# Order of the first stage, the sums of squares and the ones row in a two-layer hybrid encoder step on one Trainium2 core

## The chip, the cores and the metric

The program runs on one core of a Trainium2 chip. The core has TensorE (matrix products, two clock levels, 1.2 and 2.4 GHz), VectorE, ScalarE, GpSimd and SyncE (which issues transfers), an on-chip memory of 128 partitions (SBUF), and an accumulator memory of eight banks (PSUM) that TensorE writes. The metric is device microseconds of one execution.

## The reference

One inference step of two layers for 16 meta tokens, 1024 prompt tokens and 32 sample tokens. Shortened, one layer is:

```python
z = rmsnorm(x, norm_mix_g) @ w_in
c_q, c_kv, k_r, x_r, g_r = split(z)           # 768, 256, 32, 512, 512 columns
q = rmsnorm(c_q, q_norm_g) @ w_uq             # 8 heads of 64 + 32; the 32 are rotated
ckv, kpe = rmsnorm(c_kv, kv_norm_g), rope(k_r)
xc = conv_b + sum(shifted(x_r, k) * conv_w[k] for k in range(4))
r, i = sigmoid(xc @ w_gate_a + b_gate_a), sigmoid(xc @ w_gate_x + b_gate_x)
a = exp(-8 * r * softplus(-lam))
h_t = a_t * h_(t-1) + sqrt(1 - a_t**2) * i_t * xc_t
y = h * gelu(g_r)
o = softmax(q @ keys, chunk-causal) @ values  # keys and values from ckv, kpe and the past
x = x + concat(rmsnorm(o, attn_out_g), rmsnorm(y, lru_out_g)) @ w_out
x = x + square(relu(rmsnorm(x, norm_mlp_g) @ w_up)) @ w_down
```

After the second layer a last rmsnorm gives the outputs; new latent rows, rotary keys and states are outputs too.

## The kernel before

The 1074 columns (1072 tokens and two of padding) stand in the free dimension throughout: x is eight tiles of 128 x 1074 (`xall`). A product with K = 1024 is made from eight tiles k. Each float32 operand is split into a high and a low half, and each product runs three passes (high by high, high weight by low x, low weight by high x) over three chunks of 358 columns: 72 matmuls (`product`, L525).

Weights come in blocks of 128 x 1024. SyncE loads block b into `raw[b % 2]` (512 KB), ScalarE copies it to `whi[b % 2]` (`split`, L766) and VectorE subtracts to get `wlo[b % 2]` (L1079 in the layer's first part, L1452 in the MLP). The products are numbered units; unit u writes PSUM slot u % 2 (three banks), and may start only when unit u - 2 has been read (`take` and the table `READ`). Every engine's program is one list written by hand; engines meet only at counted semaphores. SyncE's list is a queue too: a transfer that waits holds all behind it.

A layer runs in this order. (1) A sum of squares of x: TensorE multiplies the summed squares `msq` by a tile of ones (`norm_sum`, L538), ScalarE takes the root (`root`), VectorE the reciprocal (`rstd`, L1083); every sum is a unit of its own and takes a slot. (2) Products XR0 to XR3, each followed on VectorE by `scaled` (PSUM times the reciprocal, L1089) and a convolution (L1105 to L1111). (3) Gate products (`gates`, 2 x 9 matmuls for each of four tiles c), between them GR0 to GR3 (inputs of gelu), CKV0, CKV1, KR and CQ0; for each tile VectorE runs `xc_lo`, `lru` (a reciprocal L1125, two scans L1133 and L1134), and `gelu`, with a cube on GpSimd. (4) CQ1 to CQ5, then their low halves (`lo`, L1096), then UQ0 to UQ5 (54 matmuls each), of which the last two are the rotary ones (`rotate`). (5) Keys (K, four units of 18 matmuls) and values (V, L627). (6) Eight heads in two slots of operands, even and odd (`qe`, `keh`, `kel`; `qo`, `koh`, `kol`): row maxima (L602), which become a row of shifts carried to the operands by transfers (`qe<-mt`), scores (L669), exponentials on ScalarE (L958), and products with the values (L654). VectorE's copies for head h + 2 are `load_hi` (L1317); the lru group's norm (`y_root`, `y_norm`) lies in heads 0 and 1. A row of ones in the keys multiplies the shift row; GpSimd sets it, and zeros around it, in each slot (L1553, L1575, L1577). (7) Output products OY0 to OY7 (36 matmuls, from y), a sum of squares between the third and the fourth, then OO0 to OO7 (from attention). (8) MLP, four groups of 16 units; in the last, x's tiles get their next halves `xgh` (L1032), `xgl` and squares.

The sum of the MLP's norm already lies outside the slots before: in PSUM banks 6 and 7 and in the rest of a slot.

## Time and profile before

| | us |
|---|---|
| median of 3 runs | 2854.16 |
| the three runs | 2854.16, 2854.26, 2852.26 |
| the profiled execution | 2850.93 |
| its span, first to last instruction | 2848.9 |
| TensorE busy | 2684.7 (94%) |
| VectorE busy | 1303.5 (46%) |
| ScalarE busy | 813.6 (29%) |
| mean granted clock of TensorE | 0.979 |

Busy time is time in which an engine runs an instruction; for TensorE it doesn't tell at which clock. Times in the rows below count from the span's start. Engines are named PE, DVE, ACT, POOL and SP there, L525 is a line of the kernel, "x360" a count of instructions, and names stand without buffer numbers.

### The profile page before, as it was taken

How to read it: one execution, taken by the hardware profiler on the slowest of the kernel's cores; microseconds unless marked ns; L12 is line 12 of the kernel's file. 1: busy time of each engine (PE TensorE's matmuls, PEld its weight loads, DVE VectorE, ACT ScalarE, POOL GpSimd, SP SyncE). 2: the span in 40 equal slices, each digit the busy share in tenths (PEclk: the TensorE clock that was granted, in tenths of full speed). 3: DMA queues.
4: the chain of work that ended last, by engine and by line, in shares of the span. 5: the costliest groups of instructions: out<-in, count | busy, mean ns of one | idle time of the engine just before them, and what ended most of it. 6: DMA issues, size and time to landing. Idle time of an engine off the chain costs nothing.

```text
span 2848.9 us, 37082 instructions
## 1 busy us (share of the span) xinstructions
PE 2684.7 (94%) x15742; PEld 2582.5 (91%) x15742; DVE 1303.5 (46%) x1425; ACT 813.6 (29%) x1235; POOL 353.1 (12%) x230
## 2 busy tenths in 40 slices
PE   6899989999999999999999998899999999999995
PEld 5889967899999999999989887778999999999995
DVE  7785666565223223223378855764542232222334
ACT  3342245533202112022223333454321120220221
POOL 0022243211000000000201323341200000000011
PEclk9999999999999999999999999999999999999998
DMA  5111200211111111111221111002111111111122
GB/s 189 45 51 57 68 9 18 79 56 49 45 45 45 45 45 45 45 45 58 80 69 45 63 45 53 9 33 78 52 45 45 45 45 45 46 45 45 45 76 93
DMA packets 46114, 152.48 MB, mean 54 GB/s; under 512 B 8849, under 2 KB 10033, under 8 KB 45953
## 3 DMA queue, kind: packets, MB, share of 16 engines
q1 hardware_dynamic: 38576, 128.69, 13.8%
q0 software_dynamic: 5792, 15.86, 1.4%
q10 hardware_dynamic: 1584, 5.54, 0.5%
q8 instruction: 132, 2.16, 0.3%
q14 instruction: 30, 0.24, 0.0%
HBM read 127.48 MB, written 20.24 MB: 52 GB/s over the span
## 4 chain that ended last, share of the span: by engine, by line
PE 85%; DVE 6%; ACT 3%; issue 2%; POOL 2%; DMA 2%; SPq 0%; DVEq 0%; ACTq 0%; POOLq 0%
PE ps L725 53%; PE ps L525 20%; PE ps L654 5%; PE ps L669 4%; PE ps L602 2%; DVE t L1125 1%; PE ps L627 1%; PE ps L538 1%; POOL t L1520 1%; DMA qo<-mt 0%; DVE wlo L1079 0%; DVE xc L1133 0%; DMA comp<-sum_scratch 0%; DVE xc L1111 0%; ACT t L786 0%
## 5 line engine op out<-in xcount | busy, mean ns | idle before, releaser
L1452 DVE TENSOR_TENSOR wlo<-raw,whi 128x1024 fp32r<-128x1024 f32 x124 | 151.9, 1225 | 901.0 <-ACT whi L1019 900.9
L1019 ACT ACTIVATE whi<-raw 128x1024 fp32r<-128x1024 f32 x124 | 131.5, 1060 | 973.1 <-PE ps L725 972.8
L725 PE MATMUL ps<-xmh,whi 128*128 128x358 f32 x1536 | 336.2, 327 | 2.7 <-issue 2.7
L725 PE MATMUL ps<-xml,whi 128*128 128x358 f32 x1536 | 336.8, 327 | 0.0
L725 PE MATMUL ps<-fh,whi 128*128 128x358 f32 x1536 | 336.4, 327 | 0.0
L725 PE MATMUL ps<-fh,wlo 128*128 128x358 f32 x1536 | 336.3, 327 | 0.0
L725 PE MATMUL ps<-xmh,wlo 128*128 128x358 f32 x1536 | 335.5, 326 | 0.0
L725 PE MATMUL ps<-fl,whi 128*128 128x358 f32 x1536 | 335.1, 326 | 0.0
L725 PEld LDWEIGHTS ps<-xmh,whi 128*128 128x128 f32 x1536 | 264.4, 189 | 3.8 <-issue 3.8
L725 PEld LDWEIGHTS ps<-fl,whi 128*128 128x128 f32 x1536 | 266.6, 189 | 0.0
L725 PEld LDWEIGHTS ps<-fh,whi 128*128 128x128 f32 x1536 | 265.9, 189 | 0.0
L725 PEld LDWEIGHTS ps<-xmh,wlo 128*128 128x128 f32 x1536 | 265.8, 189 | 0.0
L725 PEld LDWEIGHTS ps<-fh,wlo 128*128 128x128 f32 x1536 | 265.0, 189 | 0.0
L725 PEld LDWEIGHTS ps<-xml,whi 128*128 128x128 f32 x1536 | 264.5, 189 | 0.0
L525 PE MATMUL ps<-xgh,whi 128*128 128x358 f32 x816 | 184.2, 335 | 21.8 <-ACT t L786 21.8
L1497 POOL DMA_DIRECT2D x_scratch<-xall x24 | 13.5, 562 | 1481.3 <-DVE xall L1470 1464.4
L525 PE MATMUL ps<-xgl,whi 128*128 128x358 f32 x816 | 181.6, 331 | 0.0
L525 PE MATMUL ps<-xgh,wlo 128*128 128x358 f32 x816 | 180.8, 330 | 0.0
L1328 DVE TENSOR_REDUCE mxp<-ps 64x1 f32<-64x64 f32 (+11 forms) x384 | 141.2, 372 | 84.1 <-PE ps L602 77.5
L525 PEld LDWEIGHTS ps<-xgh,whi 128*128 128x128 f32 x816 | 143.8, 194 | 25.5 <-issue 24.9
L1462 DVE TENSOR_TENSOR fl<-msq,fh 128x1074 fp32r<-128x1074 f32 x64 | 81.8, 1278 | 147.4 <-ACT fh L1027 147.4
L766 ACT ACTIVATE whi<-raw 128x1024 fp32r<-128x1024 f32 (+3 forms) x80 | 74.8, 935 | 249.5 <-PE ps L525 249.2
(260 smaller groups left out, 4034.0 us busy)
## 6 DMA issues: line engine op xcount, KB each, us to landing
raw<-in_wst SPq DMA_DIRECT2D x204, 512.0 KB, 3.3
x_scratch<-xall POOLq DMA_DIRECT2D x24, 537.0 KB, 3.8
xall<-x_scratch ACTq DMA_DIRECT2D x10, 537.0 KB, 6.2
xall<-in_xT SPq DMA_DIRECT2D x8, 537.0 KB, 8.1
out_yT<-xall SPq DMA_DIRECT2D x8, 537.0 KB, 3.7
rc<-sum_scratch SPq DMA_DIRECT2D x16, 268.0 KB, 4.0
xall<-x_scratch SPq DMA_DIRECT2D x6, 537.0 KB, 4.6
ra<-qr SPq DMA_DIRECT2D x16, 134.2 KB, 2.4
```

The source lines that it names most:

```text
L525: mm = nc.tensor.matmul(dst(q), wt, r(q), start=(k == 0 and i == 0), stop=(k == n - 1 and i == 2))
L538: mm = nc.tensor.matmul(ps[:, 3 * (u % 2) + q, 0:CH], ones[:, :], tile[:, q * CH:(q + 1) * CH], start=True, stop=True)
L602: mm = nc.tensor.matmul(ps[:, max_bank(h, s), c0:c0 + n], qs[e][0][rows, q0:q0 + P], ks[e][0][rows, k0:k0 + n], start=True, stop=True, ski ...
L627: mm = nc.tensor.matmul(ps[:, t % 3, :], (ckvh if a == "h" else ckvl)[k][:, c0:c0 + P], (whi if c == "h" else wlo)[B_UV % 2][:, 512 * k:51 ...
L654: mm = nc.tensor.matmul(ps[0:65, bank, c0:c0 + n], v[:, v0:v0 + 65], p_tile(gk)[:, 0:n], start=(k in FIRST), stop=(k in LAST))
L669: mm = nc.tensor.matmul(ps[:, gi % 3, 0:n], ks[e][0 if a == "h" else 1][rows, k0:k0 + P], qs[e][0 if c == "h" else 1][rows, q0:q0 + n], st ...
L725: mm = nc.tensor.matmul(ps[:, 3 * (u % 2) + q, 0:CH], wt, (rh if c == "h" else rl)[kk](q), start=(kk == 0 and i == 0), stop=(kk == 7 and i ...
L766: nc.scalar.activation(whi[b % 2][:, 0:n], raw[b % 2][:, 0:n], ACT.Copy).then_inc(S["w_hi"], 1)
L1019: nc.scalar.activation(whi[b % 2][:, :], raw[b % 2][:, :], ACT.Copy).then_inc(S["w_hi"], 1)
L1328: ins = V.reduce_max(mxp[lo_:hi_, tile, part:part + 1], ps[lo_:hi_, max_bank(h, s), c0:c0 + n], AX_X)
L1452: V.tensor_tensor(wlo[b % 2][:, :], raw[b % 2][:, :], whi[b % 2][:, :].bitcast(F32), ALU.subtract).then_inc(S["w_lo"], 1)
L1462: V.tensor_tensor(fl[k][:, :], msq[:, :], fh[k][:, :].bitcast(F32), ALU.subtract).then_inc(S["f_lo"], 1)
```

## The change

It has six parts. (a) In layer 0 SyncE issues x's tiles first, the first two weight blocks among them and the constants behind them; XR0 and XR1 run interleaved, tile by tile, as x's low halves come; x isn't stored at the start and is read from the input again for the residual. In layer 1 the first two blocks are loaded and split in the MLP's last group, and XR0 doesn't wait for the sum. (b) All sums of squares lie outside the slots, in banks 6 and 7 (`sum_of`), each behind another product: MIX behind XR1 (layer 0) or XR0 (layer 1), KV behind CQ1, Y behind CQ4, Q behind UQ1, O behind OY4. (c) The order is XR0 to XR3, GR0, GR1, gates 0, GR2, GR3, gates 1, CKV0, CKV1, gates 2, KR, CQ0, gates 3, CQ1 and on; the four convolution inputs have tiles of their own, `lru` is cut in two with the next tile's `xc_lo` between, the rotary query units come first, and y is normalised before attention. (d) VectorE sets the ones and zeros in the rotary keys' tile `kpe`, and they reach both slots with the copies of its rows; GpSimd's settings in the key slots go. (e) The eight transfers of rotated queries stand among the loads of blocks 28 to 30. (f) The last layer makes no next halves of x and stores no x.

The diff, cut to what the parts below speak of:

```diff
-B_XR, B_GR, B_CKV, B_KR = [0, 1, 2, 3], [5, 6, 8, 9], [11, 12], 14
-B_GATE = [4, 7, 10, 13]
-B_CQ = [15, 16, 17, 18, 19, 20]
+B_XR, B_GR, B_CKV, B_KR = [0, 1, 2, 3], [4, 5, 7, 8], [10, 11], 13
+B_GATE = [6, 9, 12, 15]
+B_CQ = [14, 16, 17, 18, 19, 20]
...
+U_XR, U_GR, U_GATE, U_CKV = [0, 1, 2, 3], [4, 5, 8, 9], [6, 10, 14, 18], [12, 13]
+U_KR, U_CQ = 16, [17, 20, 21, 22, 23, 24]
+U_UQ, U_K, U_V = [25, 26, 27, 28, 29, 30], 31, 35
+U_OY, U_OO, U_MLP = [45 + _c for _c in range(8)], 53, 61
...
+SUM_MIX, SUM_KV, SUM_Y, SUM_Q, SUM_O, SUM_MLP = 1, 2, 3, 4, 5, 6
+SUM_AT = {SUM_KV: U_CQ[1], SUM_Y: U_CQ[4], SUM_Q: U_UQ[1], SUM_O: U_OY[4], SUM_MLP: U_MLP}
...
+            for m in range(8):
+                sp.dma_start(x[m], xT[m]).then_inc(S[f"x_load{m}"], 16)
+                if m < 2:
+                    sp.dma_start(raw[m][:, :], wst[m]).then_inc(S[f"raw{m}"], 16)
             sp.dma_start(ones[:, :], ident_in[1]).then_inc(S["const_in"], 16)
             sp.dma_start(ident[:, :], ident_in[0]).then_inc(S["const_in"], 16)
             sp.dma_start(fg[:, :], fgain).then_inc(S["const_in"], 16)
...
-                w("mm", U_SMIX + 1)
+                def load(b):
+                    w("w_lo", b)
+                    sp.dma_start(raw[b % 2][:, :], wst[L * NB + b]).then_inc(S[f"raw{b % 2}"], 16)
+                if L:
+                    for n in (0, 1):
+                        sp.wait_ge(S["w_lo"], L * NB + n)
+                        sp.dma_start(raw[n][:, :], wst[L * NB + n]).then_inc(S[f"raw{n}"], 16)
+                    sp.wait_ge(S["xg_hi"], L * 8 + 8)
+                    sp.wait_ge(S["xg_lo"], L * 8 + 8)
+                    sp.dma_start(vecs[:, :], vec[L]).then_inc(S["vec_in"], 16)
+                sp.dma_start(h0s[:, :], h0[L]).then_inc(S["small_in"], 16)
+                sp.dma_start(xs[:, :, 0:CW - 1], conv0[L]).then_inc(S["small_in"], 16)
+                sp.dma_start(past[:, :, :], past_ckv[L]).then_inc(S["small_in"], 16)
+                w("sum", SUM_MIX)
                 sp.dma_start(cosT[:, :], ropeC).then_inc(S["table_in"], 16)
                 sp.dma_start(sinT[:, :], ropeS).then_inc(S["table_in"], 16)
-                with sp.Fori(1, 15) as i:
+                with sp.Fori(1, 14) as i:
...
+                def sum_of(n, tile):
+                    if n > 1 or L:
+                        pe.wait_ge(S["root"], L * PER["root"] + n - 1)
+                    for q in range(2):
+                        nc.tensor.matmul(ps[:, 6 + q, :], ones[:, :], tile[:, 512 * q:512 * q + 512], start=True, stop=True)
+                    nc.tensor.matmul(sum_rest(slot_of(sum_at(n, L))), ones[:, :], tile[:, SUM_END:T], start=True, stop=True).then_inc(S["sum"], 1)
+                pe.wait_ge(S["const_in"], 48)
...
+                if L == 0:
+                    for k in range(8):
+                        x_ready(k)
+                        for c in (0, 1):
+                            if k == 0:
+                                w("w_lo", B_XR[c] + 2)
+                            dst = to_slot(U_XR[c])
+                            for i, (a, b) in enumerate(PASSES):
+                                wt = (whi if a == "h" else wlo)[B_XR[c] % 2][:, 128 * k:128 * k + 128]
+                                for q in range(3):
+                                    mm = nc.tensor.matmul(dst(q), wt, (XH if b == "h" else XL)[k](q), start=(k == 0 and i == 0), stop=(k == 7 and i == 2))
+                            if k == 7:
+                                mm.then_inc(S["mm"], 1)
+                    mix_sum()
+                else:
+                    product(to_slot(U_XR[0]), U_XR[0], B_XR[0], 0, XH, XL, x_ready)
+                    mix_sum()
+                    product(to_slot(U_XR[1]), U_XR[1], B_XR[1], 0, XH, XL)
+                def x_product(u, b):
+                    product(to_slot(u), u, b, 0, XH, XL)
+                for c in (2, 3):
+                    x_product(U_XR[c], B_XR[c])
+                for c in (0, 1):
+                    x_product(U_GR[c], B_GR[c])
                 gates(0)
+                for c in (2, 3):
+                    x_product(U_GR[c], B_GR[c])
+                gates(1)
                 for c in (0, 1):
-                    product(to_slot(U_GR[c]), U_GR[c], B_GR[c], 0, XH, XL)
-                gates(1)
-                for c in (2, 3):
-                    product(to_slot(U_GR[c]), U_GR[c], B_GR[c], 0, XH, XL)
+                    x_product(U_CKV[c], B_CKV[c])
                 gates(2)
-                for c in (0, 1):
-                    product(to_slot(U_CKV[c]), U_CKV[c], B_CKV[c], 0, XH, XL)
+                x_product(U_KR, B_KR)
+                x_product(U_CQ[0], B_CQ[0])
                 gates(3)
-                product(to_slot(U_KR), U_KR, B_KR, 0, XH, XL)
-                product(to_slot(U_CQ[0]), U_CQ[0], B_CQ[0], 0, XH, XL)
+                x_product(U_CQ[1], B_CQ[1])
...
+                sum_of(SUM_KV, sqa)
+                for c in (2, 3, 4):
+                    x_product(U_CQ[c], B_CQ[c])
+                w("y_sum", 3)
+                sum_of(SUM_Y, t3)
+                x_product(U_CQ[5], B_CQ[5])
...
-                        if i == 3:
-                            w("o_sum", 3)
-                            norm_sum(U_SO, osq)
                         product(to_slot(U_OY[i]), U_OY[i], B_OY + bi, 512 * n, [tok(t) for t in yh], [tok(t) for t in yl],
                                 (lambda k: w("y_lo", k + 1)) if i == 0 else None)
+                        if U_OY[i] == SUM_AT[SUM_O]:
+                            w("o_sum", 3)
+                            sum_of(SUM_O, osq)
...
+                def root(n, dst, dim):
+                    w("sum", n)
+                    nc.scalar.activation(dst[:, 0:SUM_END].rearrange("p (c n) -> p c n", c=2), ps[:, 6:8, :], ACT.Sqrt, scale=1.0 / dim, bias=eps[:, 0:1])
+                    nc.scalar.activation(dst[:, SUM_END:T], sum_rest(slot_of(sum_at(n, L))), ACT.Sqrt, scale=1.0 / dim, bias=eps[:, 0:1]).then_inc(S["root"], 1)
...
+                V.memset(kpe[32:33, :], 1.0)
+                V.memset(kpe[96:97, :], 1.0).then_inc(S["kpe_ones"], 1)
...
+                    V.tensor_tensor(g[c][:, :], g[c][:, :], t3[:, :], ALU.mult).then_inc(S["y_n"], 1)
...
-                        if h == 0 and i in (14, 16, 18):
-                            y_root((i - 14) // 2)
-                        if h == 1 and i in (15, 16, 17, 18):
-                            y_norm(i - 15)
...
-                rstd(rs, 5)
+                split(32)
                 add_y(3)
-                split(32)
+                add_y(4)
+                rstd(rs, SUM_O)
+                split(33)
+                add_y(5)
                 for j in range(4):
                     V.tensor_tensor(o[j][:, :], o[j][:, :], rs[:, :], ALU.mult).then_inc(S["o_n"], 1)
-                add_y(4)
-                add_y(5)
-                split(33)
+                    if j == 0:
+                        split(34)
...
+                            if L < DEPTH - 1:
+                                nc.scalar.activation(xgh[m][:, :], x[m], ACT.Copy, scale=col(V_GNEXT + m)).then_inc(S["xg_hi"], 1)
...
-                w("mm", U_V + 10)
-                for k in range(2):
-                    G.memset(ks[1][k][32:64, :].bitcast(F32), 0.0).then_inc(S["slot1_set"], 1)
-                    w("slot1_set", 3 + k)
-                G.memset(ks[1][0][32:33, :].bitcast(F32), 1.0).then_inc(S["slot1_set"], 1)
-                w("slot1_set", 5)
+                for part in range(2):
+                    G.memset(qs[1][part][32:64, :].bitcast(F32), 0.0).then_inc(S["slot1_set"], 1)
+                    w("slot1_set", part + 1)
```

The rotary tables (`cosT`, `sinT`) are loaded behind the MIX sum in both, since `sinT` lies where the squares lay.

What the order of instructions shows. First SyncE's queue at the start; `xall` is x, `raw_49` and `raw_50` are the two buffers for weight blocks, `ones`, `ident` and `fg` the constants, `rope_87` and `rope_88` the rotary tables. Before:

```order
L406 DMA ones<-in_consts 128x128
L407 DMA ident<-in_consts 128x128
L408 DMA fg<-in_fgain 128x8
L410 DMA xall<-in_xT 128x1074 x8
L419 DMA raw_49<-in_wst 128x1024 [waits w_lo]
L419 DMA raw_50<-in_wst 128x1024 [waits w_lo]
...
L429 DMA rope_87<-in_ropeC 128x1074 [waits mm]
L430 DMA rope_88<-in_ropeS 128x1074
...
L434 DMA raw_49<-in_wst 128x1024
```

After:

```order
L425 DMA xall<-in_xT 128x1074
L427 DMA raw_49<-in_wst 128x1024
L425 DMA xall<-in_xT 128x1074
L427 DMA raw_50<-in_wst 128x1024
L425 DMA xall<-in_xT 128x1074 x6
L428 DMA ones<-in_consts 128x128
L429 DMA ident<-in_consts 128x128
L430 DMA fg<-in_fgain 128x8
...
L454 DMA rope_87<-in_ropeC 128x1074 [waits sum]
L455 DMA rope_88<-in_ropeS 128x1074
...
L459 DMA raw_49<-in_wst 128x1024
```

The constants move behind x and two blocks; the third block stays behind the tables, which wait for the sum.

Second, VectorE's list for one round of gates; `wlo` is a weight's low half, `xcs_96<-xc_74` the low half of the next convolution result, `g_82<-ps,rs` a scaled product, the reciprocal and what follows it the recurrence. Before, around the recurrence of tile 0:

```order
L1079 TENSOR_TENSOR wlo_53<-raw_49,whi_51 128x1024
L1094 TENSOR_TENSOR xcs_96<-xc_73,xcs_95 128x1074
L1124 TENSOR_SCALAR t_77<-t_76 128x1074
L1125 RECIPROCAL t_77<-t_77 128x1074
L1127 TENSOR_SCALAR t_76<-t_77 128x1074
...
L1133 SCALAR_TENSOR_TENSOR xc_72<-t_76,t_79 128x1040
...
L1079 TENSOR_TENSOR wlo_54<-raw_50,whi_52 128x256
L1089 TENSOR_TENSOR g_80<-ps,rs 128x1074
L1089 TENSOR_TENSOR g_81<-ps,rs 128x1074
L1079 TENSOR_TENSOR wlo_53<-raw_49,whi_51 128x1024
```

After:

```order
L1166 TENSOR_TENSOR wlo_53<-raw_49,whi_51 128x256
L1176 TENSOR_TENSOR g_80<-ps,rs 128x1074
L1166 TENSOR_TENSOR wlo_54<-raw_50,whi_52 128x1024
L1176 TENSOR_TENSOR g_81<-ps,rs 128x1074
L1166 TENSOR_TENSOR wlo_53<-raw_49,whi_51 128x1024
L1217 TENSOR_SCALAR t_77<-t_76 128x1074
L1218 RECIPROCAL t_77<-t_77 128x1074
L1181 TENSOR_TENSOR xcs_96<-xc_73,xcs_95 128x1074
L1223 TENSOR_SCALAR t_76<-t_77 128x1074
...
L1229 SCALAR_TENSOR_TENSOR xc_72<-t_76,t_79 128x1040
```

The scaled products of the first GR pair move ahead of the first recurrence, with a weight split between the two, and the next tile's low half moves into the recurrence.

Third, GpSimd's list around the first shift rows (`qe<-mt`); `koh` and `kol` are the odd slot's keys, `qo` its queries. Before:

```order
L1569 MEMSET qo 32x1074 [waits p_zero]
L1571 MEMSET qo 32x1074 [waits slot1_set]
L1575 MEMSET koh 32x1296 [waits mm,slot1_set]
L1575 MEMSET kol 32x1296 [waits slot1_set]
L1577 MEMSET koh 1x1296 [waits slot1_set]
L1586 DMA qe<-mt 1x2x16 [waits mt_lo,slot1_set]
L1587 DMA qe<-mt 1x2x32
```

After:

```order
L1689 MEMSET qo 32x1074 [waits p_zero]
L1689 MEMSET qo 32x1074 [waits slot1_set]
L1698 DMA qe<-mt 1x2x16 [waits mt_lo,slot1_set]
L1699 DMA qe<-mt 1x2x32
```

The three settings of the odd slot's keys, of which the first waits for the last product of V, are gone from ahead of the transfer.

## Rows read from the trace of the kernel before

**Rows 1.** The page, busy us of each engine, share of the span, instructions.

```profile
PE 2684.7 (94%) x15742; PEld 2582.5 (91%) x15742; DVE 1303.5 (46%) x1425; ACT 813.6 (29%) x1235; POOL 353.1 (12%) x230
```

**Rows 2.** TensorE's waits: what ended them, us in total, times, longest us.

```profile
PE ps L538 <- DVE msq L1061: 28.4, 1, 28.4
PE ps L525 <- ACT t L786: 21.8, 6, 7.0
PE ps L602 <- issue: 18.8, 8, 3.4
PE ps L669 <- DMA qe<-mt: 15.7, 4, 7.5
PE ps L525 <- DVE cql L1096: 13.1, 4, 3.8
```

**Rows 3.** The chain of waits: start, us, what.

```profile
2.15 4.25 DMA xall<-in_xT
...
32.21 47.53 PE ps L525 x288
...
213.41 59.31 PE ps L525 x360
...
290.16 1.81 PE ps L538 x6
291.97 44.45 PE ps L525 x270
...
386.08 1.38 PE ps L654 x2
407.50 3.38 issue
...
432.20 2.53 issue
...
576.59 2.08 PE ps L538 x6
578.67 76.93 PE ps L525 x468
...
1419.63 1.19 ACT xgh L1032
...
1475.73 1.28 DVE t L1089
```

**Rows 4.** Windows: length, busy us of five engines, granted clock, DMA share, GB/s.

```profile
281.00:285.00 4.00, 4.00 (x15) 4.00 (x16) 4.00 (x4) 4.00 (x5) 0.00 (x0) 0.57 0.02 3
149.71:180.44 30.73, 27.16 (x163) 26.64 (x163) 26.06 (x19) 14.65 (x14) 6.15 (x2) 1.00 0.16 51
290.00:338.00 48.00, 48.00 (x285) 46.68 (x283) 27.49 (x17) 11.58 (x12) 6.30 (x3) 1.00 0.17 55
```

**Rows 5.** Transfers of the first 40 us: GB/s in slices of 1 us, one issue group.

```profile
GB/s 0 32 136 134 284 412 370 408 387 266 296 309 425 421 421 425 417 412 421 410 425 414 430 411 412 425 417 421 300 26 129 0 0 159 279 412 388 369 16 0
...
raw<-in_wst SPq DMA_DIRECT2D x3, 512.0 KB, 16.9
```

**Rows 6.** Timeline of SyncE, the first rotary table's issue.

```profile
32.24 0.33 SPq L429 DMA_DIRECT2D rope<-in_ropeC  x1
```

**Rows 7.** Timeline of VectorE, recurrence of the second tile.

```profile
130.84 6.87 DVE L1125 RECIPROCAL t<-t 128x1074 f32<-128x1074 f32 x1
...
142.18 3.10 DVE L1133 TENSOR_TENSOR_SCAN xc<-t,t 128x1040 f32<-128x1040 f32 x1
145.21 2.46 DVE L1134 TENSOR_TENSOR_SCAN xc<-t,h0s,t 128x34 f32<-128x34 f32 x1
```

**Rows 8.** Timelines of GpSimd and ScalarE between values and scores.

```profile
375.54 1.74 POOL L1575 MEMSET koh<- 32x1296 f32 x1 [11.59 <-PE ps L627]
...
378.36 1.06 ACT L766 ACTIVATE whi<-raw 128x1024 fp32r<-128x1024 f32 x1
```

**Rows 9.** Timeline of VectorE, four tiles of attention output normalised.

```profile
588.59 4.83 DVE L1427 TENSOR_TENSOR o<-o,rs 128x1074 f32<-128x1074 f32 x4
```

More of the change, by code:

```diff
@@ L139 @@
 Y_AT = [3, 6, 9, 14]
-DVE_CHAIN = 82
+DVE_CHAIN = 87
 VTILES = [P * t for t in range(10)]
@@ L267, in trunk @@
         xc = tiles("xc", "F", 0, 4)
-        t1, t2, t3 = tiles("t", "F", 4, 3)
-        t4 = place("t4", "F", 7 * TB, T + 16)
+        tp = [place(f"t{i + 1}", "F", (4 + i) * TB + 64 * i, T + 16) for i in range(4)]
+        t1, t2, t3 = (tp[i][:, 0:T] for i in range(3))
+        t4 = tp[3]
+        xr = [tp[3], tp[0], tp[1], tp[2]]
         g = tiles("g", "G", 0, 4)
@@ L408, in _ @@
             sp.dma_start(fg[:, :], fgain).then_inc(S["const_in"], 16)
-            for m in range(8):
-                sp.dma_start(x[m], xT[m]).then_inc(S[f"x_load{m}"], 16)
             for L in range(DEPTH):
@@ L507, in take @@
                 def take(u):
-                    if u >= 2:
+                    if u in U_XR[0:2]:
+                        if L:
+                            pe.wait_ge(S["res_add"], L * PER["res_add"] - 1 + u)
+                        return
+                    if u == U_XR[2] and L == 0:
+                        w("xr_raw", 1)
+                    else:
                         w(*READ[u - 2])
+                    for n in range(1, 7):
+                        if sum_at(n, L) == u - 2:
+                            w("root", n)
                 def product(dst, u, b, woff, rhs_h, rhs_l, ready=None):
@@ L531, in to_slot, with mix_sum, x_ready @@
                 def to_slot(u):
[L532 to L546 removed]
+                    return lambda q: ps[:, 3 * slot_of(u) + q, 0:CH]
+                def sum_of(n, tile):
[5 more added lines that the diff above has]
+                pe.wait_ge(S["const_in"], 48)
+                XH, XL = [tok(t) for t in xgh], [tok(t) for t in xgl]
+                def mix_sum():
+                    pe.wait_ge(S["sq_sum"], L * 7 + 7)
+                    sum_of(SUM_MIX, msq)
+                def x_ready(k):
+                    w("xg_lo", k + 1)
                 def gates(c):
@@ L567, in _ @@
                 w("ckv_sum", 1)
-                norm_sum(U_SKV, sqa)
-                for c in range(1, 6):
-                    product(to_slot(U_CQ[c]), U_CQ[c], B_CQ[c], 0, XH, XL)
+                sum_of(SUM_KV, sqa)
[4 more added lines that the diff above has]
+                x_product(U_CQ[5], B_CQ[5])
                 for m in range(6):
@@ L697, in _ @@
                 FH, FL = [tok(t) for t in fh], [tok(t) for t in fl]
-                def mlp_sum():
-                    w("xm_sum", 7)
-                    for q in range(2):
-                        nc.tensor.matmul(ps[:, 6 + q, :], ones[:, :], msq[:, 512 * q:512 * q + 512], start=True, stop=True)
-                    nc.tensor.matmul(sum_rest(U_MLP % 2), ones[:, :], msq[:, SUM_END:T], start=True, stop=True).then_inc(S["mlp_sum"], 1)
                 def mlp_group(gg, first):
@@ new lines, in _ @@
+                scaled(U_KR, kpe[:, 0:T], rs, "kr_ev")
+                scaled(U_CQ[0], cq[0], rs, "cq_ev")
+                split(16)
+                gelu(2)
+                split(17)
+                lru_a(3)
+                lru_b(3)
+                w("root", SUM_KV)
+                scaled(U_CQ[1], cq[1], rs, "cq_ev")
+                split(18)
+                rstd(sqt, SUM_KV)
+                split(19)
+                scaled(U_CQ[2], cq[2], rs, "cq_ev")
+                gelu(3)
+                V.tensor_copy(hbuf[:, 3, 1:2], xc[3][:, TOK - 1:TOK]).then_inc(S["hid_out"], 1)
@@ L1230, in _ @@
                         .then_inc(S["ckv_n"], 1)
+                scaled(U_CQ[3], cq[3], rs, "cq_ev")
+                split(20)
+                w("table_in", 32)
+                w("kr_ev", 1)
+                rotate(kpe[:, 0:T], t1[:, :], "kpe_new")
                 w("ckv_n", 2)
-                scaled(U_CQ[1], cq[1], rs, "cq_ev")
                 for c in range(2):
@@ L1448, in mlp_group @@
                     for k in range(2 * GT):
-                        if not (last and k >= 2 * GT - 2):
+                        if not (last and L == DEPTH - 1 and k >= 2 * GT - 2):
                             b = B_MLP + k + 2
@@ L1497, in save_x @@
                 pool.dma_start(x_scr[m], x[m]).then_inc(S["x_out"], 16)
-            for m in range(8):
-                pool.wait_ge(S[f"x_load{m}"], 16)
-                save_x(m)
             for L in range(DEPTH):
```

479 lines of the change are left out of this document (241 added, 238 removed).

## The prediction

> **What bounds the kernel now.** I read the page first: TensorE is busy for 94% of the span [rows 1], so the kernel is a string of products with gaps, and a change of order can win only the gaps and what follows them. The view of TensorE's waits says what ends them [rows 2]: 28.4 us before the first sum of squares, 21.8 us in six waits for gate results from ScalarE, 18.8 us of "issue" (behind VectorE's copies ahead of a head), 15.7 us for the shift rows and 13.1 us for the low halves of the compressed queries. The chain of waits puts times to the stages [rows 3]. One product with K = 1024 is 72 matmuls: 59.31 us / 360 x 72 = 11.86 us; a gate product (9) is 1.48, an up-projection of queries (54) 8.9, a sum of squares at full clock 1.81. The granted clock adds to each gap: in the four microseconds from 281, right behind a gap, it was 0.57, near the lower of the two levels, 1.2 of 2.4 GHz [rows 4]. So a gap of about 3 us costs (1 - 0.57) x 4 = 1.7 us more.
>
> **Front, layer 0.** The new order puts x0 first on SP's queue and the constants behind all of x and two weight blocks. Before, x0 lands 4.25 us after its issue [rows 3]; issued at 0.76 it lands at about 5.0. Before, the bus moves 410 to 425 GB/s from microsecond 12 to 27 [rows 5]; eight x tiles and two blocks are 5.3 MB, 1.3 us each: the last x lands near 16.9, the constants at 17.2. TensorE waits for these first, so the early tiles buy no early start. That they queue behind is shown by the weight blocks of before, issued behind x: 16.9 us to landing, where 3.3 to 4 is usual [rows 5]. This speaks against the part of the change that puts x first. The Trainium skill, "DMA: Bandwidth & Descriptors", Queues, rings and completion order, speaks against it too: descriptors of one ring start in order, and only between queues does an engine take turns. By it the constants would come at 17.2 as well.
> The interleaved products are 144 matmuls, 23.7 us, from 17.2, plus 1.7 for the clock: they end at 42.6. x's low halves don't bind: the addition behind the last of them ended at 28.4 [rows 2], and two splits more (2.4) against an earlier start leave it there. The sum ends at 44.5.
> Here a new wait comes. Block 2 is loaded behind the two rope tables, which wait for the sum (the sine table lies where the squares lay). Before, the tables are issued at 32.24 [rows 6] and the three transfers end in the slice from 38 to 39 [rows 5], 5.8 us after; then the block lay beside products 0 and 1. Now nothing is left to hide it: it lands at 50.3, ScalarE's copy (1.06 [rows 8]) and VectorE's difference of about the same length give 52.6. TensorE waits 8.1 us, another 2 us for the clock, and two products end the stage at 78.4; before, 32.21 + 47.53 = 79.7 [rows 3]. **Gain 1.3 us** of the 28.4.
>
> **Front, layer 1.** From the last residual addition before (1418.3) to the end of the fourth product (1475.7) are 57.4 us [rows 3]. Now product 0 starts at once, the sum ends after 13.7, product 1 after 25.5. The block lands at 19.5, but the free slot needs the scaled result: ScalarE copies the block, loads a table and takes the root (23.3), VectorE inverts (6.9, as the reciprocal of the same shape [rows 7]) and scales, 31.4. Waiting 5.9 and 2 for the clock: products 2 and 3 end at 57.0. **Gain 0.4 us.**
>
> **Gates to first query product.** From the end of product 3 to the end of the first query product before: 290.16 - 79.7 = 210.4 us. The work is 13 x 11.86 + 8 x 1.48 + 8.9 = 174.9 us; after, two sums at 1.81 (KV and Y) join: 178.5. Gate products now follow two products each, so sigmoid, root, scan and scaling of one round lie beside 23.7 us of products. VectorE's work of such a round is 26.06 us busy in the row of before that holds one of each kind [rows 4], TensorE's 2 x 11.86 + 2.96 = 26.7. So it is nearly a tie: I count a first wait of 2.2 (a weight split stands ahead of the scaling that frees a slot) and 0.3 and 0.5 in two rounds: 181.3. The low halves of the first two query tiles are made early and don't delay the first query product. **Gain 29.1 per layer**: the waits of the gates, of the query halves and of a sum, and their clock. The sixth sum of squares costs the same wherever it runs; outside the slots only its waits go.
> In the tie GpSimd matters: beside its cube a scan of 34 columns takes 2.46 us, and that of 1040 columns 3.10 [rows 7]. The cube runs beside the scans in the new order too.
>
> **Queries to attention.** UQ1 to UQ5 are 44.45 us [rows 3]; one sum between instead of two: **1.8 per layer**. The rotary units come first, so the rotation and its eight copies lie beside four products. From the first key product (338.2) to the first product with the values (386.08) are 47.9 us. The wait of 3.3 us in it ("issue", the copies of head 0 behind the second rotation) goes with its clock, 5.0. At the end GpSimd sets two tiles of the odd slot, 1.74 for the first, and one row, from 375.54 on [rows 8], and only then issues the shift rows that TensorE waits 7.5 us for [rows 2]. With the ones carried by the key rows these go; late next is ScalarE, which has an eviction, two copies and a split up to 379.4 [rows 8] before its table load and the first exponentials. That leaves 6.0 of 10.7 us. **Gain 9.7 per layer.**
> In attention, y's reciprocals and products stood ahead of the copies for heads 2 and 3; their waits, 3.38 and 2.53 [rows 3], go with 1.7 each, less 1 for what the copies still take: **8.3 per layer**. They now lie beside query products, where VectorE has 27.5 of 48 us of work by the row [rows 4].
>
> **Output.** Here I expect a loss. The sum of the attention output moves from behind the third to behind the fifth product of OY. Before, the third product ends 2.9 us ahead of that sum (576.59), the sum at 578.67, and products run on without a gap for 76.93 us [rows 3]: reciprocal, normalising (4.83 for four tiles [rows 9]) and low halves lie beside five products of 5.93 (36 matmuls), the last of which ends at 608. Now the sum follows two products at once: 573.7 + 11.9 + 1.8 = 587.4; root 1.2 and reciprocal 6.9 end at 595.5. Then VectorE has an addition, four normalisings, a split that waits for the seventh product (599.2) and one more addition, so the first low half comes near 608.5, while OY ends at 605.2. The wait of 3.3 with its clock against the 2.9 that go: the first product of OO ends at 616.1, before at 613.9. **Loss 2.2 us in layer 0, 1.2 in layer 1**, where the removed wait is some 0.5 longer and its sum ran slower. Tail: the copy of 1.19 us [rows 3] leaves the chain ahead of the last sum: **gain 1.2**.
> No store of x at the start and none in the last layer: nothing waits for them but bandwidth, priced above.
>
> **Sum.** 1.3 + 0.4 + 2 x (29.1 + 1.8 + 9.7 + 8.3) - 3.4 + 1.2 = 97.3 us. Against the profiled execution's 2850.93: 2753.6. The median of the runs shown lies 3.2 above that one; so 2756.8, and 1 more for small waits in the tie: **2758**.
>
> **Bounds of the unknown.** The front's wait lies between nothing (products not held) and 8.1 + 2 + 5.9 + 2, -18 to 0 on the sum; the gate rounds between no wait, -6, and one of 2 us with its clock in three rounds of both layers, +22; the output's two waits between 0 and 8 us each, -4 to +10.
>
> **Rivals.**
> A: the constants don't hold the first products. For: they are small (two of 64 KB). Against: the queue's order above. The products would start at 12.7 (second weight split), paced by themselves: 36.4, everything to the fourth product 6.2 earlier: 2752.
> B: VectorE becomes the bound in the gate rounds. For: 26.06 against 26.7, and hand-overs between engines are no busy time. Against: the row's time holds the slow scans. Each round then costs 2 us and 1.8 of clock: 6 x 3.8 = 23, 2781.
> C: slower than before. Short waits at each gate pair hold TensorE at the lower level. In a stretch at 1.2 GHz the work takes twice its time, so it decides once 95 us of full-speed work, more than half the 178 us of one layer's gate stage, runs low: 2855 and over. For it: every gap of 3 us before was followed by a clock near half. Against: it was 0.57 only in 4 us, and the whole round from 149.7 was at 1.00 [rows 4].
> D: the interleaved products run at the lower level throughout, 47.4 us instead of 25.4, if they come in short bursts as x's low halves arrive: 22 us later, 2780. For it: a tile's copies on VectorE take 2.4 us or more, its six groups of products 3.0, so an early start would be paced. Against: TensorE is held till 17.2, when half of the tiles are ready. The Trainium skill, "TensorE: Matmul & The Clock Gate", HAM oscillation, states that waits between short bursts put the engine back to the slower clock each time.
> E: waits only move, as the output's does, and half of the 97 us comes back: 2806.
>
> **How the numbers follow.** Forecast near 2758 0.58; A 0.13; B 0.14; D 0.03; E 0.09; C 0.02; no change 0.01. The range 2746 to 2785 holds forecast, A, B and D, and takes the front's bound; outside it I leave E and C. A measurement tells about 0.2%, 6 us, from no change: faster 0.97, same 0.01, slower 0.02.
>
> **What would show it.** Right: the first matmul near 17, a gap of 8 us before product 2 in layer 0 and of 6 in layer 1; no gate wait over 2.5 us; nothing by "issue" at heads 2 and 3; the first value product 37 to 39 us after the first key product; a new wait of 3 to 5 us at the first product of the attention output. Wrong: a first matmul before 14 (A), waits for scaled results in each gate round (B), records at half clock beyond 10 us (C). It fails as a whole if the softmax start is held by what I don't see at ScalarE, or if block loads fall behind elsewhere.

## The result and the profile after

The changed kernel takes 2770.75 us (median of 4 runs, 2768.59 to 2774.17), the kernel before 2853.21 beside it: ratio 0.9714, 95% interval [0.9697, 0.9731]. The gain is 82.5 us between the medians. The forecast was 2758, the range 2746 to 2785. The profiled execution took 2772.09 us with a span of 2769.9; the granted clock is 0.987 on average, 0.979 before.

The chain of waits of the changed kernel, at the places that the prediction speaks of (start, us, what):

```profile
7.12 10.59 DMA fg<-in_fgain
17.75 26.66 PE ps L607 x144
44.41 1.72 PE ps L576 x4
47.48 5.78 DMA raw<-in_wst
53.28 1.06 ACT whi L830
54.44 1.24 DVE wlo L1166
55.72 50.22 PE ps L562 x288
...
108.34 1.20 DVE g L1176
109.67 94.44 PE ps L562 x567
...
258.63 2.58 DVE cql L1183 x2
...
265.01 2.77 DVE wlo L1166
...
352.50 1.38 PE ps L722 x2
...
566.62 1.26 DVE ol L1183
568.02 50.10 PE ps L562 x288
...
1407.53 7.03 issue
```

Against [rows 3]: the first product starts at 17.75 and not at 32.21, held by the last constant (`fg`); behind the first sum the chain runs through block 2's load, its copy and its difference, and product 2 starts at 55.72. The gate rounds are one piece of 94.44 us with one wait of 2.27 ahead of it. The first product of OO waits for a low half (`ol`).

TensorE's waits (what ended them, us in total, times, longest):

```profile
PE ps L607 <- DMA fg<-in_fgain: 17.7, 1, 17.7
PE ps L562 <- DVE wlo L1166: 11.2, 3, 9.4
PE ps L562 <- DVE ol L1183: 8.8, 2, 4.4
PE ps L562 <- issue: 7.0, 1, 7.0
PE ps L722 <- ACT pd L1046: 4.8, 2, 2.4
...
PE ps L562 <- DVE g L1176: 4.5, 2, 2.3
PE ps L562 <- DVE cql L1183: 4.1, 4, 1.6
```

Of [rows 2] the 21.8 us for gate results, the 18.8 of "issue" ahead of heads and 14.1 of the 15.7 for the even slot's shift rows are gone or nearly so (1.6 are left in this kernel's list), and the 13.1 for low halves (`cql`) are down to 4.1. New are 9.4 and 7.0 ahead of product 2, 4.4 ahead of OO and 2.4 for exponentials (`pd`) in each layer.

By stage, from the ends and starts of products in TensorE's timeline (differences in us, taken before rounding, the prediction's in brackets):

| stage | layer 0 | layer 1 |
|---|---|---|
| to the end of XR3 | 79.7 to 82.2: +2.5 (-1.3) | 57.4 to 59.0: +1.6 (-0.4) |
| XR3 to the end of UQ0 | 210.4 to 184.7: -25.7 (-29.1) | 210.5 to 184.7: -25.8 (-29.1) |
| UQ0 to the first key product | 47.7 to 47.4: -0.3 (-1.8) | 47.7 to 47.4: -0.3 (-1.8) |
| keys to the first value product | 48.2 to 38.1: -10.0 (-9.7) | 48.2 to 38.1: -10.0 (-9.7) |
| heads, to OY0 | 169.7 to 161.6: -8.1 (-8.3) | 169.8 to 159.5: -10.3 (-8.3) |
| OY and OO | 99.7 to 103.8: +4.1 (+2.2) | 101.8 to 103.8: +2.0 (+1.2) |
| MLP | 762.8 to 763.9: +1.1 (0) | 762.7 to 764.3: +1.7 (0) |
| tail | | 32.4 to 31.2: -1.2 (-1.2) |

Before rounding they add to -78.9, the difference of the two spans. The first row of layer 0 is the least certain: with the same products and loads there, it took 79.7 to 82.2 us in eight profiles (this one and those of e3 to e8 and e10; layer 1 took 58.3 to 59.0), so its +2.5 is the upper end of 0 to 2.5.

### The profile page after: what moved, and what is told of

It is laid out like the page before. It is cut to its first block, busy times and chain, and to the rows that moved or that the text cites. A ratio compares the mean times of both kernels' runs of the same rounds, so it can differ in the third digit from the quotient of the medians.

```text
span 2769.9 us, 37058 instructions
## 1 busy us (share of the span) xinstructions
PE 2668.4 (96%) x15742; PEld 2570.7 (93%) x15742; DVE 1297.4 (47%) x1425; ACT 811.4 (29%) x1240; POOL 327.9 (12%) x192
## 4 chain that ended last, share of the span: by engine, by line
PE 91%; DVE 5%; DMA 1%; issue 1%; ACT 1%; SPq 0%; POOL 0%; DVEq 0%; POOLq 0%; ACTq 0%
PE ps L786 55%; PE ps L562 22%; PE ps L722 5%; PE ps L737 4%; PE ps L671 1%; PE ps L696 1%; PE ps L607 1%; PE ps L576 1%; DVE wlo L1166 1%; DVE cql L1183 1%; DVE rs L1170 0%; DVE t L1170 0%; DMA fg<-in_fgain 0%; DVE xall L1519 0%; DVE o L1539 0%
## 5 line engine op out<-in xcount | busy, mean ns | idle before, releaser
L562 PE MATMUL ps<-xgh,whi 128*128 128x358 f32 x768 | 170.5, 330 | 16.5 <-DVE wlo L1166 9.4
L562 PE MATMUL ps<-xgl,whi 128*128 128x358 f32 x768 | 170.2, 330 | 0.0
L562 PE MATMUL ps<-xgh,wlo 128*128 128x358 f32 x768 | 169.4, 329 | 0.0
L562 PEld LDWEIGHTS ps<-xgh,whi 128*128 128x128 f32 x768 | 133.6, 192 | 17.1 <-DVE wlo L1166 9.6
L1166 DVE TENSOR_TENSOR wlo<-raw,whi 128x1024 fp32r<-128x1024 f32 (+3 forms) x76 | 101.9, 1341 | 73.6 <-ACT whi L830 73.1
```

Of the source, the lines that this page charges most:

```text
L562: mm = nc.tensor.matmul(dst(q), wt, r(q), start=(k == 0 and i == 0), stop=(k == n - 1 and i == 2))
L1166: V.tensor_tensor(wlo[b % 2][:, 0:n], raw[b % 2][:, 0:n], whi[b % 2][:, 0:n].bitcast(F32), ALU.subtract).then_inc(S["w_lo"], 1)
```

## The experiments

All are the changed kernel with an edit, timed beside the kernel before, whose median lay between 2851.1 and 2852.5 in these sets. The gain of an edit is taken from the ratios against 0.9714; both ratios have an interval of 0.0017 to either side, some 4.8 us, so for edits of 4 to 7 us the stage in the trace carries the reading.

**e1_block_first**: the third weight block ahead of the sum and the tables.

```diff
+                load(2)
                 w("sum", SUM_MIX)
                 sp.dma_start(cosT[:, :], ropeC).then_inc(S["table_in"], 16)
                 sp.dma_start(sinT[:, :], ropeS).then_inc(S["table_in"], 16)
-                with sp.Fori(1, 14) as i:
+                load(3)
+                with sp.Fori(2, 14) as i:
```

> The changed kernel with the load of block 2 ahead of the wait for the sum and of the two rope tables, and block 3 right behind the tables. My theory: the 9.4 us before product 2 in layer 0 and the 7.0 us in layer 1 are the block's late landing (in layer 1 the copy of it stands ahead of the root on ScalarE). Then product 2 follows the sum at once in both layers; 1.4 us of waiting come back ahead of product 3; with 2.8 and 2.6 us of lower clock the gain over the changed kernel's 2770.75 is 17 to 21 us, near 2752. Rival: the scaled results (root, reciprocal) set the start of products 2 and 3 anyway, the wait moves behind product 2 and the gain is under 6 us.

Ratio 0.9645 [0.9629, 0.9662], 2749.86 us: 19.7 us gained. The chain of this kernel at the sum:

```profile
43.71 1.72 PE ps L578 x4
45.42 0.16 PE ps L579 x2
45.58 11.93 PE ps L564 x72
```

Product 2 follows the sum without a gap, and layer 1 has none there either; no wait took its place ahead of product 3. To the end of XR3 12.5 and 9.6 us go; from there to UQ0 1.6 come back in each layer, so that the first two stages are 11.0 and 8.1 us shorter. The wait of 2.27 us on `g`, which this edit leaves, is followed by a lower clock here and not in the changed kernel (the last section has both rows).

My theory that the block was last, and not the scaled result, holds in layer 0 only. In layer 1 of the changed kernel product 2 waits for its slot, as the prediction has it, and the late block makes that late through ScalarE, where its copy stands ahead of the root:

```profile
1402.57 1.06 ACT L830 ACTIVATE whi<-raw 128x1024 fp32r<-128x1024 f32 x1 [8.56 <-DMA raw<-in_wst]
1404.94 1.12 ACT L835 ACTIVATE rs<-ps,eps 128x1024 f32<-128x1024 f32 x1
1413.18 2.46 DVE L1176 TENSOR_TENSOR t<-ps,rs 128x1074 f32<-128x1074 f32 x2
```

The block's low half is ready at 1404.96, the first of the two scalings near 1414.4, and product 2 starts at 1414.56. Moving the block shortens both ways.

**e2_const_late**: TensorE awaits the constants at the first sum.

```diff
-                pe.wait_ge(S["const_in"], 48)
                 XH, XL = [tok(t) for t in xgh], [tok(t) for t in xgl]
                 def mix_sum():
+                    pe.wait_ge(S["const_in"], 48)
                     pe.wait_ge(S["sq_sum"], L * 7 + 7)
```

> The changed kernel, but TensorE waits for the constants at the first sum of squares and not before the first product. My theory: only the constants hold the first product till 17.75 us; without that wait the first product starts at 9.9 us, the second at 12.8, and products 0 and 1 end between 36 and 39 us instead of 44.4, since VectorE's low halves come every 2.44 us against 2.97 us of products: 6 to 8 us gained, 2763 to 2765. Rival (D of the prediction): paced by x's arrival, TensorE stays at the lower clock through the interleaved products (47 us of them instead of 24), and the end moves to 50 us or later: no gain, or 5 to 12 us lost.

Ratio 0.9692 [0.9676, 0.9708], 2764.06 us: 6.3 us gained. TensorE's first wait:

```profile
PE ps L607 <- DVE wlo L1143: 10.1, 1, 10.1
```

The first product starts at 10.1 us and the 144 matmuls end at 36.0, in 25.9 us, against 26.7 from 17.75: pacing by arrival did not hold TensorE at the lower clock (rival D), and the products ended 8.4 us earlier. The wait for block 2 stayed (9.6), and the stage to XR3 took 73.5 us, 6.3 to 8.7 less than in the eight profiles named above.

**e3_osum_early**: the output sum behind the fourth product of OY; ScalarE's splits of blocks 33 and 34 move with VectorE's.

```diff
-SUM_AT = {SUM_KV: U_CQ[1], SUM_Y: U_CQ[4], SUM_Q: U_UQ[1], SUM_O: U_OY[4], SUM_MLP: U_MLP}
+SUM_AT = {SUM_KV: U_CQ[1], SUM_Y: U_CQ[4], SUM_Q: U_UQ[1], SUM_O: U_OY[3], SUM_MLP: U_MLP}
...
                 add_y(3)
-                add_y(4)
                 rstd(rs, SUM_O)
-                split(33)
-                add_y(5)
+                add_y(4)
                 for j in range(4):
                     V.tensor_tensor(o[j][:, :], o[j][:, :], rs[:, :], ALU.mult).then_inc(S["o_n"], 1)
                     if j == 0:
-                        split(34)
+                        split(33)
+                        add_y(5)
                 add_y(6)
+                split(34)
```

> The changed kernel with the sum of squares of the attention output behind the fourth product of OY instead of the fifth, VectorE's reciprocal and low halves moved up with it. My theory: the 4.4 us before the first product of OO in both layers are this chain's lateness; one product (5.9 us) earlier is enough, the squares are ready at that place, and with the lower clock behind the waits (3.4 and 1.7 us) the gain is 11 to 14 us, near 2758. Rival: the squares on GpSimd are not ready a product earlier, and a wait of 2 to 3 us before the sum takes the place: gain 3 to 6 us.

Ratio 0.9673 [0.9657, 0.9689], 2757.67 us: 11.7 us gained. Its chain:

```profile
531.07 6.14 PE ps L562 x36
537.21 1.72 PE ps L576 x4
538.92 0.16 PE ps L577 x2
539.08 26.93 PE ps L562 x164
```

The squares are ready at the fourth product's end, and OO follows OY without a wait: the stage is 97.8 and 97.5 us, 6.2 and 6.4 less than in the changed kernel and 2.0 and 4.5 less than before the change.

**e4_gate_split**: the scaling of GR1 ahead of a split.

```diff
-                split(7)
                 scaled(U_GR[1], g[1], rs, "gr_ev")
+                split(7)
                 split(8)
```

> The changed kernel with the scaling of GR1 ahead of the split of block 7 on VectorE. My theory: the 2.27 us before gates 0 in each layer are the split that stands ahead of the scaling which frees the slot; swapped, they go, nothing else moves: 4 to 5 us gained, near 2766. Rival: the split is then late for GR2, and a wait of 1 to 2 us takes its place there: gain 1 to 2 us.

Ratio 0.9699 [0.9683, 0.9715], 2764.73 us: 4.3 us, within the interval of the changed kernel. In its trace the two waits of 2.27 on `g` are gone, and in each layer a wait of 0.58 for ScalarE's reading of a gate result has come at GR2; from XR3 to UQ0 1.4 us go in each layer (184.7 to 183.3). So the stage bears out 2.8 us, between theory and rival; the rival's wait came, shorter and from another engine.

**e5_head_work**: extra VectorE work at the old places of y's norm.

```diff
+                        if h == 0 and i in (14, 16, 18):
+                            q = (i - 14) // 2
+                            link(V.reciprocal(rs[:, q * CH:(q + 1) * CH], rs[:, q * CH:(q + 1) * CH]))
+                        if h == 1 and i in (15, 16, 17, 18):
+                            link(V.tensor_tensor(rs[:, :], rs[:, :], rs[:, :], ALU.max))
```

> The changed kernel with VectorE work of the old y_root and y_norm put back at their old places in heads 0 and 1, on a tile that nothing reads then (three reciprocals of 358 columns, four operations of 1074); y itself stays normalised early, so this is extra work that prices the place. My theory: the old waits ahead of heads 2 and 3 (3.4 and 2.5 us, and about 1.7 of lower clock each) come back in both layers: 15 to 19 us slower than the changed kernel, near 2787. Rival: with the rest of the order changed the heads have slack, and the cost is under 5 us.

Ratio 0.9791 [0.9775, 0.9807], 2791.28 us: 22.0 us lost, 10.1 and 11.2 of it in the heads of the two layers. The waits of before are back:

```profile
PE ps L671 <- issue: 13.0, 7, 3.7
```

3.72 us ahead of head 2 and 2.54 ahead of head 3, as in [rows 3], and a stretch at the lower clock follows each. The heads alone differ by some 3 us between versions that don't touch them (158.4 to 161.6), so the 21.4 us agree with the 18.4 that the change gained there, and with the 16.6 forecast.

**e6_memsets_back**: settings on GpSimd ahead of the first shift rows (the counts of `slot1_set` that others wait for go from 2 to 6).

```diff
+                w("mm", U_V + 10)
+                for part in range(4):
+                    G.memset(rs[32 * part:32 * part + 32, :], 0.0).then_inc(S["slot1_set"], 1)
+                    w("slot1_set", 3 + part)
```

> The changed kernel with GpSimd settings of about the old length (four of 32 x 1074 on a tile that nothing reads then, some 1 us each, in place of two of 1.74 and a row of 1.2) behind the last product of V and ahead of the first shift rows. My theory: the shift rows come 4 to 5 us later, TensorE waits 6 to 8 us for them as before, and the first product with the values moves by 4 to 5 us in each layer: 8 to 12 us slower than the changed kernel. Rival: ScalarE, whose copies end 3 us after V, sets the start of attention in either case: under 3 us.

Ratio 0.9751 [0.9735, 0.9768], 2780.31 us: 10.6 us lost, 5.2 and 5.8 between keys and values. TensorE's wait for the shift rows:

```profile
PE ps L737 <- DMA qe<-mt: 16.9, 3, 8.6
```

Two of the three are the first scores of a layer (8.0 and 8.6). It is the 15.7 us of [rows 2] again: GpSimd's settings were what held attention's start.

**e7_tie**: one VectorE operation more per recurrence.

```diff
+                    link(V.scalar_tensor_tensor(out=t3[:, :], in0=t3[:, :], scalar=1.0, in1=t3[:, :], op0=ALU.mult, op1=ALU.max))
                     V.tensor_tensor_scan(xc[c][:, 0:STREAM], t1[:, 0:STREAM], t4[:, 0:STREAM], 0.0, ALU.mult, ALU.add)
```

> The changed kernel with one more VectorE operation of 1.27 us in each recurrence (t3 = max(t3, t3), which changes nothing), eight in all. My theory that VectorE and TensorE nearly tie in the gate rounds (26.2 us busy in a round of 26.7): each round after the first gets longer by about what is added less 0.5, 0.8 us and small clock effects: 4 to 10 us slower than the changed kernel. Rival: VectorE has slack that its busy time doesn't show (it idles only for lack of work): under 2 us.

Ratio 0.9756 [0.9739, 0.9772], 2780.61 us: 12.0 us lost for 10.2 us of added work in the two layers. Its waits at the gates and at the first query product:

```profile
PE ps L562 <- DVE cql L1183: 6.1, 2, 3.1
PE ps L562 <- DVE g L1176: 5.1, 4, 2.3
...
PE ps L562 <- DVE ckv L1176: 2.9, 2, 1.4
...
PE ps L562 <- DVE kpe L1176: 2.0, 2, 1.0
```

A wait now stands at each later round (0.3, 1.4 and 1.0 us), one of 1.0 at y's sum, and the rest ahead of the first query product. To UQ0 6.5 and 6.4 us are lost; 0.8 come back behind it. VectorE has little slack from the gates to UQ0: the tie was real, and the changed kernel stays just on the good side of it.

**e8_y_late**: y's reciprocal behind the split of UQ2's block.

```diff
                 split(21)
-                rstd(t3, SUM_Y)
                 cq_low(2)
...
                 split(23)
+                rstd(t3, SUM_Y)
                 for c in range(4):
```

> The changed kernel with the reciprocal of y's norm (6.9 us on VectorE) moved from between the low halves of the compressed queries to behind the split of UQ2's block. My theory: VectorE, busy 37 of 39 us ahead of the first query product, makes its waits (1.6, 0.5 and 0.9 us); without the reciprocal there they go, and the query products have room for it: 5 to 6 us gained in two layers. Rival: the query products have no such room, since y's normalisation, the second reciprocal and two rotations then come late: waits of 3 us and more ahead of UQ4 or the key products, no gain or a loss.

Ratio 0.9696 [0.968, 0.9712], 2765.68 us: 5.1 us, again about the interval. The waits on `cql` fall from 4.1 to 0.9 us, and from the first query product to the keys 59.1 us become 57.2 in both layers: the stage bears out 3.8. Of the three waits that I put down to the reciprocal only the first, 1.6 us, goes; those of 0.5 and 0.9 (the latter at UQ1, for a weight's low half) stay. UQ1's split takes 2.85 us on VectorE, beside a multiplication on GpSimd, where one of the same shape takes 0.95 without; from the changed kernel:

```profile
250.87 0.95 DVE L1166 TENSOR_TENSOR wlo<-raw,whi 128x768 fp32r<-128x768 f32 x1
264.93 2.85 DVE L1166 TENSOR_TENSOR wlo<-raw,whi 128x768 fp32r<-128x768 f32 x1
264.71 2.25 POOL L1633 TENSOR_TENSOR sqa<-sqa,sqa 128x1074 f32<-128x1074 f32 x1 [9.39 <-ACT sqa L927]
```

The 1.9 us more would cover the wait of 0.9; no run moved that multiplication.

**e10_gates_first**: gates 0 ahead of GR0 and GR1. Only TensorE's part is shown; blocks, units and the lists of ScalarE and VectorE change with it.

```diff
+                gates(0)
                 for c in (0, 1):
                     x_product(U_GR[c], B_GR[c])
-                gates(0)
```

> The changed kernel with the gate products of tile 0 directly behind XR3, ahead of GR0 and GR1, as before the change (blocks, units and the lists of ScalarE and VectorE renumbered to fit; tile 0's recurrence then lies ahead of the scaling of GR0 and GR1). My theory: the two products in front of gates 0 are what covers the four convolutions; without them TensorE waits 10 to 16 us for the convolutions and the first gate result, with 3.4 us of lower clock, in each layer, and later rounds give back 2 to 4: 16 to 30 us slower than the changed kernel. Rival: VectorE bounds the whole stage, so the order of the first pair is worth little: under 8 us.

Ratio 0.9827 [0.9811, 0.9843], 2801.37 us: 32.2 us lost, a little more than I expected. Its waits:

```profile
PE ps L562 <- ACT t L851: 22.2, 2, 11.6
...
PE ps L562 <- DVE xcs L1181: 5.8, 2, 3.2
```

In each layer 3 us pass before the first gate product and 10.6 to 11.6 before GR0, until the fourth convolution is done and ScalarE has read the first gate; from XR3 to UQ0 15.9 and 15.5 us are lost. Nothing is given back later. The pair of products in front of the gates, with the lists that go with it, is worth some 60% of the 25.7 us that the whole stage gained.

**e9_all**: the edits of e1, e2, e3, e4 and e8 together.

> Five edits together: block 2 ahead of the tables, constants awaited at the first sum, the output sum a product earlier, the scaling of GR1 ahead of the split, y's reciprocal late. My theory: they lie in different stages and add: 19.7 + 6.3 + 11.7 + 4.3 + 5.5 = 47.5 us against the changed kernel, ratio to the kernel before 0.955 (2723 where that one takes 2852). Rival: the earlier front uncovers the convolutions or the gate rounds, as VectorE nearly ties there, and 8 to 15 us of the sum come back as waits at the gates.

Ratio 0.9545 [0.9529, 0.9561], 2722.14 us: 48.2 us below the changed kernel, where the five single gains add to 47.1, each with its interval. They do not quite add by place: the 1.6 us per layer that e1 loses behind the wait on `g` are not lost here, since e4's edit removes that wait (XR3 to UQ0 takes 181.5 us in both layers, where the single differences give 183.1). The longest waits that are left:

```profile
PE ps L609 <- DVE wlo L1146: 10.3, 1, 10.3
PE ps L803 <- POOL msq L1718: 4.7, 1, 4.7
PE ps L724 <- ACT pd L1048: 4.6, 2, 2.4
```

**e11_v_to_exp** and **e12_split_14**: e9 with less of ScalarE's work between the values and the first exponential; in e12 the split of block 30 later still.

```diff
+                    if t == 3:
+                        w("qr", 2)
+                        qn_hi(1)
...
                 kslot_hi(1)
-                w("qr", 2)
-                qn_hi(1)
-                split(30)
...
+                    if gi == 6:
+                        split(30)
```

> The five edits of e9 and one more: between the values and the first exponential ScalarE no longer copies head 1's queries (done during V) nor block 30 (done after the seventh pair of head 0). My theory: ScalarE's 5.9 us between the last value product and the first exponentials set the start of attention; 2.2 us fewer there move the first product with the values by 2 to 2.5 us in each layer: 4 to 6 us below e9. Rival: the shift rows or VectorE's copies for head 1 are just behind, gain under 2 us.

> The version of e11 with the split of block 30 on ScalarE and VectorE behind pair 14 of head 0 instead of pair 6. My theory: at pair 6 VectorE's part stood ahead of a row maximum, which gave back 1.6 us in each layer in head 0 (the heads took 0.7 and 1.2 us longer than in e9); behind the last maximum of the head it hides: 2 to 3 us below e11, near 2717. Rival: ScalarE's copy among the exponentials is what costs, and nothing is gained.

Ratios 0.9532 [0.9516, 0.9548] and 0.9535 [0.9519, 0.9551], 2719.2 and 2720.05 us. From keys to values 38.1 us become 36.1 and 36.3 in e11, so ScalarE was last there (the wait on `pd` falls from 2.4 in e9 to 1.2); but a new wait stands in head 0, where VectorE's split lies ahead of a row maximum:

```profile
PE ps L673 <- DVE mxp L1444: 3.7, 3, 1.7
```

In e12 that wait is down to 0.3, but the predicted 2 to 3 us did not come (the heads take 161.7 and 159.6 us, 162.2 and 159.8 in e11), and neither version can be told from e9 by its time.

## Why the prediction was right

Against the profiled executions the sum was 97.3 us and 78.8 were measured (2850.93 - 2772.09). The mechanisms held nearly everywhere; what is missing are sizes of terms, each with its place:

**Front.** Its mechanism held, and the waits came out longer than forecast. The constants do queue behind x (17.75, forecast 17.2; e2), and block 2 behind the tables makes the wait that takes the place of the one removed (9.4 and 7.0 us, forecast 8.1 and 5.9; e1), in layer 1 by way of the slot, as written. Forecast was a gain of 1.7 us in two layers, measured a loss of 4.1, so the sign was wrong; by the spread in the eight profiles named above, the loss lies between 0.9 and 4.1. The first 20 matmuls took 6.1 us, 0.30 each where the later ones take 0.165: the start costs 2.8 us and not 1.7. The view's granted clock reads 1.00 in that stretch, so that the clock is the reason is not shown. The sum ended 1.8 late, and the load landed 7.0 us behind the sum's end instead of 5.8. I took 5.8 from three transfers; here a fourth, block 3 (issued at 48.10), moves beside them: 307 GB/s from 47 to 54 us are 2.15 MB, where 271 from 33 to 39 were 1.63 before the change. Rival A is refuted by the row itself; its price of 6.2 agrees with the 6.3 of e2, within the interval.

**Gates to UQ0.** Forecast 29.1 per layer, measured 25.7. The first wait is the 2.2 that was named (2.27; e4). The missing 3.4 are the 2.1 us ahead of UQ0, which I had put at nothing because the first two low halves are early: the next two still queue behind y's reciprocal, which makes 1.6 of the 2.1 (e8). Products and sums that run 1% longer than the 11.86 and 1.81 taken are 1.9 more, and the 0.8 forecast for two later rounds did not come. The tie of VectorE and TensorE (26.06 against 26.7) was right and is narrow (e7); rival B did not come, with 26.24 us busy in the second round of 26.7. By e10 the cover in front of the gates is worth 15.9 and 15.5 of the 25.7; how the other 10 divide among the later order, the recurrence cut in two and the sums outside the slots was not tried.

**Queries to attention.** 10.0 for 9.7: the settings on GpSimd held the start (e6), and ScalarE is last now (e11), as forecast. UQ to keys gave 0.3 of 1.8: a weight split is 0.9 late at UQ1, and stays so without y's reciprocal ahead of it (e8); UQ1 to UQ5 take 44.8 us and not 44.45, and the sum 1.88 and not 1.81.

**Heads.** 8.1 and 10.3 for 8.3, within what this stage varies; e5 brings the two waits back.

**Output.** The new wait was forecast at 3.3 us and is 4.4; behind it the granted clock is at 0.50 for some 7 us in layer 0 and some 3 in layer 1. The loss of 4.1 and 2.0 is this term (e3).

**MLP.** I had it unchanged; it took 2.7 us more in all, the last section tells where 2.2 of them lie.

**Rivals and range.** C, D and E did not come: the changed kernel's clock is higher, and what moved into new waits is 9.4 + 7.0 + 8.8 us, of which the forecast had 20.6. One reading under C is wrong: not every gap of 3 us before was followed by a clock near half (the last section has one of 3.18 us at 1.00). That 2770.75 lies in the range is in part luck: the range was made for the front, the gate rounds and the output, and some 11 of the 18.5 us that are missing are terms that had no bound in it, the 2.1 ahead of UQ0, the 1% on the products of that stage and the MLP.

## What to carry to other kernels

A table load that waits for a result must not stand in a queue ahead of a weight block that doesn't: here the reordering of the front gave nothing until one line moved the block (19.7 us). When work is moved to cover a wait, look at the last link of the old cover: the scaling of GR1, the output's low halves and the query halves each had one product too few or one operation ahead of them, and each showed as a wait of 2 to 4.4 us on VectorE in the next profile. The five edits of e9 added up within the intervals, and where two met, in the wait on `g`, the second removed what the first had made dearer.

## What the runs showed that was not expected

The MLP's products are the same in both kernels, but those that stream the low halves `fl` got slower, in every version of the changed kernel. From the page of the kernel before and of the changed one (busy us, mean ns of one):

```profile
L725 PE MATMUL ps<-fl,whi 128*128 128x358 f32 x1536 | 335.1, 326 | 0.0
```

```profile
L786 PE MATMUL ps<-fl,whi 128*128 128x358 f32 x1536 | 337.3, 327 | 0.0
```

The other five groups differ by 0.2 us at most. The tiles of `fl` lie in a region that the change shifts by 192 bytes (the one ahead of it grew from 64 to 256 bytes of padding); `fh`, `xmh` and `xml` don't lie behind it. Whether the address is the cause was not tried.

Not every wait costs clock, and its length alone doesn't tell. In the changed kernel, windows behind the waits of 9.4 and 4.4 us and one around a wait of 2.27 (length, busy us of five engines, granted clock, DMA share, GB/s):

```profile
56.00:61.00 5.00, 5.00 (x18) 5.00 (x19) 3.06 (x1) 2.84 (x4) 0.00 (x0) 0.50 0.32 107
105.00:112.00 7.00, 4.73 (x29) 4.46 (x28) 2.41 (x2) 5.29 (x5) 0.00 (x0) 1.00 0.23 77
568.00:573.00 5.00, 4.98 (x17) 5.00 (x18) 5.00 (x5) 0.00 (x0) 0.00 (x0) 0.50 0.01 3
```

The middle one holds the wait of 2.27 us and stays at full clock. With 0.50 the granted clock is at the lower level, 1.2 GHz. In e1 the same wait of 2.27 us, 94.87 to 97.14, is followed by a lower clock; and in the kernel before, a wait of 3.18 us that ends at 180.44 is not:

```profile
97.00:101.00 4.00, 3.85 (x14) 3.89 (x15) 0.02 (x1) 2.42 (x4) 0.00 (x0) 0.57 0.36 130
177.00:186.00 9.00, 5.82 (x35) 5.45 (x34) 8.01 (x9) 7.18 (x7) 1.31 (x1) 1.00 0.35 117
```

So an edit that leaves a wait as it is can still make it dearer by some 1.6 us, as e1 did.
